# TensorE multiplies an identity by itself 112 times while it waits, in each of five normalizing stages

## The chip, the cores and the metric

The program runs on one core of a Trainium2 chip. The metric is the device time of one execution in microseconds (us), lower is better. The five engines are TensorE (PE), VectorE (DVE), ScalarE (ACT), GpSimd (POOL) and SyncE (SP, which only issues transfers here). TensorE reads its operands from SBUF and writes to PSUM, which has eight banks of 128 x 512 fp32. TensorE's clock has two levels in the profile: a granted clock of 1.00 (2.4 GHz) and of 0.50 (1.2 GHz).

## The reference

A sequence of 512 rows of 1024 numbers (`x`) passes two layers of one kind and then one of another. Everything is fp32.

```python
# each of two layers
h = rms_norm(x, norm1[l])          # x * rsqrt(mean(x*x, over a row) + 1e-6) * gain
proj = h @ w_in[l]                 # four kinds of attention read slices of proj
...
x = x + mixed @ w_out[l]
x = x + square(relu(rms_norm(x, norm2[l]) @ w_up[l])) @ w_down[l]
# then, once
shift, scale, gate = split(silu(c) @ ada_w + ada_b, 3)
h = rms_norm_2(x, norm_w) * (1.0 + scale) + shift
proj = h @ w_in_2                  # gated delta rule and dilated attention follow
```

So rows of x are normalized and multiplied by a weight matrix at five places: twice in each of the two layers, once in the last part. (A final norm of each part isn't followed by a product and uses another function.)

## The kernel before

The kernel is written in stages, one after another. A stage is a block of hand-written programs, one for each engine, with semaphores of its own. It ends in a barrier of all engines (`clear`, L196), and no engine begins the next stage before it. The two layers are a loop on the chip, so their code stands once in the program and runs twice.

Large products take fp32 operands as pairs (a rounded high part and the rest), and each product is three matmuls with 512 moving columns (`product`, L174 to L176). The weights come in items of 512 KB through a ring of four buffers (`WeightRing`). ScalarE makes the high part of an item (L144), VectorE the low part (L153), and TensorE takes both.

`norm_and_turn` is the stage that stands before those products at all five places. Its tile names differ: the rows that it scales are called `proj` (the projecting stage of each layer), `rows_mlp` (the stage ahead of the hidden layer) and `v_t` (the last part), and the pair that it makes is `turned_x`, `turned_x_mlp` and again `turned_x`. Its steps:

1. ScalarE squares the four tiles of x, 128 rows each, and sums them (L274). VectorE makes the mean (L289), ScalarE the root (L276), VectorE its reciprocal (L291).
2. VectorE scales the four tiles and raises `scaled` (L293).
3. TensorE waits for all four (`pe.wait_ge(scaled, T)`), then turns 32 blocks of 128 x 128 through the fp32 identity (L324), four into each of the eight PSUM banks, and raises `turned` once per bank.
4. ScalarE makes the high part of each bank (L280) and VectorE the rest (L298). In the last part there is a bias: VectorE first scales and shifts the bank (L312), ScalarE copies (L283), VectorE subtracts (L302).

`ident_half` is a bf16 copy of the identity, made once at the start. The attention stages use it to add masks (L396). I number the five stages 1 to 5 in the order of time: 1 and 3 are the projecting stages of the two layers, 2 and 4 the stages ahead of the hidden layer, 5 is that of the last part.

Of the kernel before, what the change touches and what calls it, by code (L numbers as in the profile page):

```python
# [32 lines left out]
P = 128  # L33
S = 512
D = 1024
T = S // P
KD = D // P
# [224 lines left out]

def norm_and_turn(nc, psum, x, xn, gains, pair, ident, small, bias=None, work=None):


    ss, ms, root, rstd = (small[:, 4 * i:4 * i + 4] for i in range(4))
    with stage(nc, "squared mean_ready root_ready dve_own scaled turned shifted high low") as (
            squared, mean_ready, root_ready, dve_own, scaled, turned, shifted, high, low), nc.Block() as block:  # L270
        @block.scalar
        def _(act):
            for t in range(T):
                act.activation(xn[:, t, :], x[:, t, :], ACT.Square, accum_out=ss[:, t:t + 1]).then_inc(squared, 1)  # L274
            act.wait_ge(mean_ready, 1)
            act.activation(root, ms, ACT.Sqrt).then_inc(root_ready, 1)  # L276
            for k in range(KD):
                if bias is None:
                    act.wait_ge(turned, k + 1)
                    act.activation(pair[:, k, 0, :], psum[:, k, :], ACT.Copy, scale=gains[:, k:k + 1]).then_inc(high, 1)  # L280
                else:
                    act.wait_ge(shifted, k + 1)
                    act.activation(pair[:, k, 0, :], work[:, k % 2, :], ACT.Copy).then_inc(high, 1)  # L283

        @block.vector
        def _(dve):
            own = Chain(dve, dve_own)
            dve.wait_ge(squared, T)
            dve.tensor_scalar(ms, ss, 1.0 / D, EPS, ALU.mult, ALU.add).then_inc(mean_ready, 1)  # L289
            dve.wait_ge(root_ready, 1)  # L290
            own(dve.reciprocal(rstd, root))  # L291
            for t in range(T):
                dve.tensor_scalar(xn[:, t, :], x[:, t, :], rstd[:, t:t + 1], None, ALU.mult).then_inc(scaled, 1)  # L293

            def rest(k):
                dve.wait_ge(high, k + 1)
                if bias is None:
                    dve.scalar_tensor_tensor(out=pair[:, k, 1, :], in0=psum[:, k, :], scalar=gains[:, k:k + 1],  # L298
                                             in1=pair[:, k, 0, :].bitcast(F32), op0=ALU.mult,
                                             op1=ALU.subtract).then_inc(low, 1)  # L300
                else:
                    dve.tensor_tensor(pair[:, k, 1, :], work[:, k % 2, :], pair[:, k, 0, :].bitcast(F32),  # L302
                                      ALU.subtract).then_inc(low, 1)

            for k in range(KD):
                if bias is None:
                    rest(k)
                    continue
                dve.wait_ge(turned, k + 1)
                if k >= 2:  # L310
                    dve.wait_ge(low, k - 1)
                dve.tensor_scalar(work[:, k % 2, :], psum[:, k, :], gains[:, k:k + 1], bias[:, k:k + 1],  # L312
                                  ALU.mult, ALU.add).then_inc(shifted, 1)
                if k >= 1:
                    rest(k - 1)
            if bias is not None:
                rest(KD - 1)

        @block.tensor
        def _(pe):  # L320
            pe.wait_ge(scaled, T)
            for k in range(KD):
                for t in range(T):
                    mm = pe.transpose(psum[:, k, t * P:(t + 1) * P], xn[:, t, k * P:(k + 1) * P], ident[:])  # L324
                mm.then_inc(turned, 1)
# [337 lines left out]
def layers(nc, psum, x, weights, consts, norm1, w_in, mla_q_norm, mla_kv_norm, mla_w_uq, mla_w_ukv,  # L663
# [8 lines left out]
    with nc.Fori(0, DEPTH) as l, ExitStack() as lay:  # L672
        def sb(name, shape, ctx=lay, dtype=F32):
            return ctx.enter_context(nc.sbuf_tensor(name, shape, dtype))
# [22 lines left out]
        gains = sb("gains", [P, 32])  # L697
# [3 lines left out]
        small = sb("small", [P, 32])  # L701
# [32 lines left out]
        with ExitStack() as mix:  # L734
            values = sb("values", [P, T, VALUES_W], mix)
            gates = sb("gates", [P, 2, S], mix)
            turned = sb("turned_qk", [P, N_TURNED, S], mix)
            with ExitStack() as ctx:
                proj = sb("proj", [P, T, PROJ_W], ctx)
                with ExitStack() as c2:  # L740
                    turned_x = sb("turned_x", [P, KD, 2, S], c2, F32R)

                    rows_x = proj[:].rearrange("p t c -> p (t c)")[:, 0:T * D].rearrange("p (t c) -> p t c", t=T)
                    norm_and_turn(nc, psum, x, rows_x, gains[:, 0:8], turned_x, ident, small)
                    in_projection(nc, psum, weights, turned_x, dict(proj=proj, values=values), turned, chunks, ends,
                                  rope, sb("sines", [P, 896], c2))
                qa = sb("qa", [P, T, 4 * MLA_DIM], ctx)
                ka = sb("ka", [P, T, 4 * MLA_DIM], ctx)
                with ExitStack() as c2:
                    latents(nc, psum, weights, proj, qa, ka, values, gates, gains, forget_bias, gate_forms, small, ident,  # L750
                            rope, sb("latent", [P, T, 384], c2), sb("latent_t", [P, 3, 2, S], c2, F32R),
                            sb("gate_work", [P, 3, S], c2))
                turn_heads(nc, psum, proj, qa, ka, turned, ident)

            chosen = sb("chosen", [P, T, S], mix)
            with ExitStack() as ctx:
                score_keys(nc, psum, values, turned, chosen, causal, sb("relu", [P, 3, S], ctx))
            mixed = sb("mixed", [P, KD, 2, S], mix, F32R)
            with ExitStack() as ctx:
                kept = sb("kept_keys", [P, T - 1, S], ctx, BF16)  # L760
                jobs = layer_jobs(turned, values, gates, kept, causal_half, window, sinks)
                stores = [(mixed[:, c, 0, :], lambda bank: bank, mixed[:, c, 1, :])
                          for g in JOB_ORDER for c in (2 * "abcd".index(g), 2 * "abcd".index(g) + 1)]
                with stage(nc, ATTENTION_SEMS) as sems:
                    attention(nc, psum, jobs, stores, ident, ident_half, sb("probs", [P, 6, S], ctx),
                              sb("probs_t", [P, 2, S], ctx), sb("o_rows", [P, 2, S], ctx),
                              sb("stats", [P, 5, len(jobs)], ctx), sems,
                              besides=(*select_keys(chosen, kept, sb("best", [P, 8], ctx)), 3 * len(jobs) // 8))
            output_products(nc, psum, x, weights, mixed, KD, len(out_items) // 2)


        with ExitStack() as ctx:
            turned_x = sb("turned_x_mlp", [P, KD, 2, S], ctx, F32R)
            with ExitStack() as c2:
                norm_and_turn(nc, psum, x, sb("rows_mlp", [P, T, D], c2), gains[:, 8:16], turned_x, ident, small)
            hidden = sb("hidden", [P, KH, 2, S], ctx, F32R)
            relu = sb("relu_mlp", [P, 3, S], ctx)
            square = sb("square_mlp", [P, 3, S], ctx)
            for half in range(2):
                half_mlp(nc, psum, x, weights, turned_x, hidden, KH, relu, square, len(down_items) // 2)  # L780
# [1397 lines left out]
def second_part(nc, psum, x, weights, consts, a):  # L2178
# [3 lines left out]
    with ExitStack() as all2:  # L2182
        def sb(name, shape, ctx=all2, dtype=F32):
            return ctx.enter_context(nc.sbuf_tensor(name, shape, dtype))
# [19 lines left out]
        small = sb("small_2", [P, 32])  # L2204
        cols = sb("cols_2", [P, 64])
        conv_cols = sb("conv_cols", [P, CONV * 3 * H])
        modulated = sb("modulated", [P, 16])
# [6 lines left out]
        with ExitStack() as ctx:  # L2214
            norm_rows(nc, x, a["final_norm"].rearrange("(o d) -> o d", o=1), sb("norm_work", [P, 3, D], ctx), small)
            work = (sb("vec_rows_2", [64, P], ctx), sb("conv_rows", [96, P], ctx), sb("silu_c", [P, KD], ctx),
                    sb("silu_pair", [P, KD, 2, P], ctx, F32R), sb("gate_bias", [P, D], ctx),
                    sb("mod_rows", [P, 2 * D], ctx))
# [3 lines left out]
        turned_x = sb("turned_x2", [P, KD, 2, S], dtype=F32R)  # L2222
# [6 lines left out]
        with ExitStack() as conv:  # L2229
# [8 lines left out]
            with ExitStack() as ctx:  # L2238
                v_t = sb("v_t", [P, H, S], ctx)
                norm_and_turn(nc, psum, x, v_t[:].rearrange("p k s -> p (k s)").rearrange("p (t c) -> p t c", t=T),  # L2240
                              modulated[:, 0:8], turned_x, ident, small, bias=modulated[:, 8:16], work=scratch)
                with ExitStack() as c2:
                    conv_projection(nc, psum, weights, turned_x, (q_t, k_t, v_t), heads_rows, conv_cols, pick, head_vecs,
                                    (sb("before", [P, 3, S + 3], c2), scratch, sb("soft", [H, 2, S], c2)), n_conv,
# [294 lines left out]
```

## Time and profile before

| | |
|---|---|
| time, median of 3 runs (lowest to highest) | 2691.14 us (2690.57 to 2691.74) |
| profiled execution: its own time | 2687.88 us |
| profiled execution: span | 2686.2 us |
| mean granted TensorE clock over the span | 0.893 |
| TensorE matmuls busy | 2238.1 us (83% of the span) |
| VectorE / ScalarE busy | 1238.2 us (46%) / 862.8 us (32%) |

The span runs from the first to the last instruction of the core, and the execution's own time has 1.7 us around it. A busy share is a mean over stages. What a change in one stage is worth must be read from that stage: which engine the barrier at its end waits for.

### The profile page before, as it was taken

Reading aid. Unit: us, or ns where it says so; the run is one execution under the profiler, and the core shown is the slowest. Engines: PE = TensorE matmul, PEld = TensorE weight load, DVE = VectorE, ACT = ScalarE, POOL = GpSimd, SP = SyncE. Lnnn points to the kernel's source line nnn. Section 1 sums busy time; section 2 is a strip of 40 time slices with the busy share of each in tenths; the row PEclk is TensorE's granted clock in tenths of the full one; section 3 lists DMA queues with packets and bytes.
Section 4 is the critical chain, followed back from the end, with each engine's and each line's share of the span. In section 5 each row is a group of like instructions: output and inputs, shape, how many; then the busy total and the mean of one; then the engine's idle time right before and its main releaser. Section 6 shows DMA issues by size and latency. Waiting matters only on the chain. (4 is left out here: it accounts for less than half of the span.)

```text
span 2686.2 us, 28827 instructions
## 1 busy us (share of the span) xinstructions
PE 2238.1 (83%) x10584; PEld 1780.0 (66%) x10588; DVE 1238.2 (46%) x2313; ACT 862.8 (32%) x1676; POOL 69.1 (3%) x75
## 2 busy tenths in 40 slices
PE   4978988999969968979999965996868785999676
PEld 3866776878857846768878854773756674776454
DVE  2458734323313568434324244665566633224343
ACT  2236423313212255423223133332223224225221
POOL 0000000000000000000000000000012210000000
PEclk9988798999989977789999987996789997998878
DMA  3310021322312300023323244221122223231121
GB/s 104 99 57 1 1 63 57 107 88 87 102 50 84 94 17 1 9 63 94 95 79 94 86 142 143 79 79 32 50 81 75 75 79 134 82 94 33 43 67 47
DMA packets 156565, 192.55 MB, mean 72 GB/s; under 512 B 20555, under 2 KB 118778, under 8 KB 156162
## 3 DMA queue, kind: packets, MB, share of 16 engines
q1 hardware_dynamic: 156418, 190.63, 23.1%
q8 instruction: 87, 1.43, 0.2%
q14 instruction: 60, 0.49, 0.1%
HBM read 178.01 MB, written 12.60 MB: 71 GB/s over the span
## 5 line engine op out<-in xcount | busy, mean ns | idle before, releaser
L153 DVE TENSOR_TENSOR weight_pairs<-weight_ring,weight_pairs 128x1024 fp32r<-128x1024 f32 (+2 forms) x313 | 377.7, 1208 | 642.3 <-ACT weight_pairs L144 641.0
L144 ACT ACTIVATE weight_pairs<-weight_ring 128x1024 fp32r<-128x1024 f32 (+2 forms) x313 | 326.5, 1045 | 803.3 <-PE psum L176 761.5
L174 PE MATMUL psum<-turned_x,weight_pairs 128*128 128x512 f32 (+1 forms) x704 | 292.1, 415 | 38.2 <-PEq L196 24.5
L176 PE MATMUL psum<-turned_x,weight_pairs 128*128 128x512 f32 (+1 forms) x704 | 285.0, 405 | 0.0
L175 PE MATMUL psum<-turned_x,weight_pairs 128*128 128x512 f32 (+1 forms) x704 | 284.1, 404 | 0.0
L174 PE MATMUL psum<-turned_x_mlp,weight_pairs 128*128 128x512 f32 x512 | 204.3, 399 | 13.0 <-PEq L196 13.0
L174 PE MATMUL psum<-weight_pairs,hidden 128*128 128x512 f32 x512 | 203.2, 397 | 0.0
L175 PE MATMUL psum<-turned_x_mlp,weight_pairs 128*128 128x512 f32 x512 | 202.4, 395 | 0.0
L176 PE MATMUL psum<-turned_x_mlp,weight_pairs 128*128 128x512 f32 x512 | 202.3, 395 | 0.0
L176 PE MATMUL psum<-weight_pairs,hidden 128*128 128x512 f32 x512 | 202.0, 395 | 0.0
L175 PE MATMUL psum<-weight_pairs,hidden 128*128 128x512 f32 x512 | 201.8, 394 | 0.0
L174 PEld LDWEIGHTS psum<-turned_x,weight_pairs 128*128 128x128 f32 (+1 forms) x704 | 136.0, 193 | 78.2 <-issue 34.3
L174 PE MATMUL psum<-weight_pairs,turned_x 128*128 128x512 f32 (+2 forms) x384 | 145.9, 380 | 21.7 <-PEq L196 11.3
L176 PEld LDWEIGHTS psum<-turned_x,weight_pairs 128*128 128x128 f32 (+1 forms) x704 | 135.0, 192 | 34.0 <-issue 0.9
L175 PEld LDWEIGHTS psum<-turned_x,weight_pairs 128*128 128x128 f32 (+1 forms) x704 | 135.9, 193 | 31.4 <-issue 0.6
L839 DVE TENSOR_TENSOR square_mlp<-relu_mlp 128x512 f32<-128x512 f32 x64 | 44.1, 689 | 222.4 <-ACT relu_mlp L820 222.4
L176 PE MATMUL psum<-weight_pairs,turned_x 128*128 128x512 f32 (+2 forms) x384 | 144.9, 377 | 0.0
L175 PE MATMUL psum<-weight_pairs,turned_x 128*128 128x512 f32 (+2 forms) x384 | 144.6, 377 | 0.0
L174 PEld LDWEIGHTS psum<-turned_x_mlp,weight_pairs 128*128 128x128 f32 x512 | 96.7, 189 | 36.6 <-issue 14.2
L176 PEld LDWEIGHTS psum<-turned_x_mlp,weight_pairs 128*128 128x128 f32 x512 | 96.8, 189 | 23.7
L176 PEld LDWEIGHTS psum<-weight_pairs,hidden 128*128 128x128 f32 x512 | 96.1, 188 | 24.1
L175 PEld LDWEIGHTS psum<-turned_x_mlp,weight_pairs 128*128 128x128 f32 x512 | 97.1, 190 | 22.2
(404 smaller groups left out, 3620.9 us busy)
## 6 DMA issues: line engine op xcount, KB each, us to landing
weight_ring<-in_w_in_dram SPq DMA_DIRECT2D x104, 512.0 KB, 3.7
weight_ring<-in_w_up_dram SPq DMA_DIRECT2D x64, 512.0 KB, 3.7
weight_ring<-in_w_down_dram SPq DMA_DIRECT2D x64, 512.0 KB, 3.7
weight_ring<-in_w_out_dram SPq DMA_DIRECT2D x24, 512.0 KB, 3.7
weight_ring<-in_ada_w_dram SPq DMA_DIRECT2D x24, 512.0 KB, 4.8
spilled<-v_t SPq DMA_DIRECT2D x22, 256.0 KB, 2.7
weight_ring<-in_w_proj_a_dram SPq DMA_DIRECT2D x8, 512.0 KB, 3.5
qk<-spilled SPq DMA_DIRECT2D x2, 2048.0 KB, 11.6
```

What stands on the lines that cost most here:

```text
L144: act.activation(self.pairs[:, i % SPLIT_RING, 0, 0:n], self.buf[:, i % RING, 0:n], ACT.Copy).then_inc(self.rounded, 1)
L153: dve.tensor_tensor(self.pairs[:, i % SPLIT_RING, 1, 0:n], self.buf[:, i % RING, 0:n], self.pairs[:, i % SPLIT_RING, 0, 0:n].bitcast(F32), ...
L174: pe.matmul(out, lhs[0], rhs[0], start=start, stop=False)
L175: pe.matmul(out, lhs[0], rhs[1], start=False, stop=False)
L176: return pe.matmul(out, lhs[1], rhs[0], start=False, stop=stop)
L839: dve.tensor_tensor(square[:, f % B, :], relu[:, f % B, :], relu[:, f % B, :], ALU.mult).then_inc(squared, 1)
```

## The change

```diff
+IDLE_PRODUCTS = 112
+
+
-def norm_and_turn(nc, psum, x, xn, gains, pair, ident, small, bias=None, work=None):
+def norm_and_turn(nc, psum, x, xn, gains, pair, ident, ident_half, small, bias=None, work=None):
...
         @block.tensor
         def _(pe):
+            for _ in range(IDLE_PRODUCTS):
+                pe.matmul(psum[:, KD - 1, 0:P], ident_half[:], ident_half[:], start=True, stop=True)
             pe.wait_ge(scaled, T)
             for k in range(KD):
                 for t in range(T):
```

The three calls pass `ident_half` on; nothing else changes. Each added matmul comes with a load of its 128 x 128 bf16 weights. All write the same 128 columns of the last PSUM bank, which the turned rows overwrite later; nothing reads them.

On TensorE, around stage 2 and stage 4 (the rows `rows_mlp`; `mixed` belongs to the stage ahead, `turned_x_mlp` with `weight_pairs` to the stage behind), the program had:

```order
L176 MATMUL psum<-weight_pairs,mixed 128x512
L630 UNCONDITIONAL_BRANCH
L319 UNCONDITIONAL_BRANCH [waits barrier_Pool_Activation_PE_DVE_SP_release]
L324 MATMUL psum<-ident,rows_mlp 128x128 [waits scaled]
L324 MATMUL psum<-ident,rows_mlp 128x128 x31
L270 UNCONDITIONAL_BRANCH
L797 UNCONDITIONAL_BRANCH [waits barrier_Pool_Activation_PE_DVE_SP_release]
L174 MATMUL psum<-turned_x_mlp,weight_pairs 128x512 [waits weights_split]
```

and now has (line numbers of the changed file, which are higher by 3 to 5):

```order
L176 MATMUL psum<-weight_pairs,mixed 128x512
L635 UNCONDITIONAL_BRANCH
L322 UNCONDITIONAL_BRANCH [waits barrier_Pool_Activation_PE_DVE_SP_release]
L325 MATMUL psum<-ident_half 128x128 x112
L329 MATMUL psum<-ident,rows_mlp 128x128 [waits scaled]
L329 MATMUL psum<-ident,rows_mlp 128x128 x31
L273 UNCONDITIONAL_BRANCH
L802 UNCONDITIONAL_BRANCH [waits barrier_Pool_Activation_PE_DVE_SP_release]
L174 MATMUL psum<-turned_x_mlp,weight_pairs 128x512 [waits weights_split]
```

The 112 products stand between the barrier's release and the wait for `scaled`, and have no wait of their own. The same row is put in at the same place of the other three stages, and the order of no other engine changes. The chip executes 560 more products in all.

## Rows read from the trace of the kernel before

**Rows 1.** The page: TensorE's busy time, and granted clock in 40 slices.

```profile
PE 2238.1 (83%) x10584; PEld 1780.0 (66%) x10588; DVE 1238.2 (46%) x2313; ACT 862.8 (32%) x1676; POOL 69.1 (3%) x75
...
PEclk9988798999989977789999987996789997998878
```

**Rows 2.** Timeline, stage 2: start, us, engine, line, operation, tiles [idle before it].

```profile
401.42 1.06 ACT L274 ACTIVATE rows_mlp<-x_stream 128x1024 f32<-128x1024 f32 x1 [7.65 <-PEq L196]
...
407.44 2.74 DVE L293 TENSOR_SCALAR rows_mlp<-x_stream,small 128x1024 f32<-128x1024 f32 x4
410.24 5.06 PE L324 MATMUL psum<-ident,rows_mlp 128*128 128x128 f32 x32 [12.06 <-DVE rows_mlp L293]
411.40 0.69 ACT L280 ACTIVATE turned_x_mlp<-psum,gains 128x512 fp32r<-128x512 f32 x1 [4.20 <-PE psum L324]
412.12 5.76 DVE L298 SCALAR_TENSOR_TENSOR turned_x_mlp<-psum,gains,turned_x_mlp 128x512 fp32r<-128x512 f32 x8 [1.93 <-ACT turned_x_mlp L280]
...
418.65 0.47 PE L174 MATMUL psum<-turned_x_mlp,weight_pairs 128*128 128x512 f32 x1 [3.35 <-PEq L196]
```

**Rows 3.** Windows of stage 2: length, busy time of each engine, then clock.

```profile
398.20:402.80 4.60, 0.00 (x0) 0.00 (x0) 2.49 (x4) 1.38 (x3) 0.00 (x0) 1.00 0.02 8
402.80:410.24 7.44, 0.00 (x0) 0.00 (x0) 3.09 (x6) 4.37 (x8) 0.00 (x0) 0.50 0.00 0
410.24:413.04 2.80, 2.80 (x13) 2.80 (x14) 0.82 (x2) 1.37 (x2) 0.00 (x0) 0.50 0.02 6
413.04:418.65 5.61, 2.26 (x22) 2.05 (x20) 4.72 (x7) 3.58 (x6) 0.00 (x0) 1.00 0.00 0
...
419.87:423.28 3.41, 3.41 (x9) 2.67 (x8) 1.14 (x1) 0.00 (x0) 0.00 (x0) 0.50 0.24 61
423.28:430.00 6.72, 6.72 (x30) 5.44 (x29) 0.00 (x0) 1.06 (x1) 0.00 (x0) 1.00 0.13 47
```

**Rows 4.** Timeline, the other four stages.

```profile
23.42 1.28 ACT L274 ACT_TABLE_LOAD   x1 [23.42 <-PEq L196]
33.54 5.66 PE L324 MATMUL psum<-ident,proj 128*128 128x128 f32 x32 [11.35 <-DVE proj L293]
35.42 5.96 DVE L298 SCALAR_TENSOR_TENSOR turned_x<-psum,gains,turned_x 128x512 fp32r<-128x512 f32 x8 [1.93 <-ACT turned_x L280]
...
809.29 6.20 DVE L298 SCALAR_TENSOR_TENSOR turned_x<-psum,gains,turned_x 128x512 fp32r<-128x512 f32 x8 [1.93 <-ACT turned_x L280]
...
1192.83 5.95 DVE L298 SCALAR_TENSOR_TENSOR turned_x_mlp<-psum,gains,turned_x_mlp 128x512 fp32r<-128x512 f32 x8 [1.93 <-ACT turned_x_mlp L280]
...
1646.60 1.06 ACT L274 ACTIVATE v_t<-x_stream 128x1024 f32<-128x1024 f32 x1 [14.83 <-PEq L196]
1655.42 5.39 PE L324 MATMUL psum<-ident,v_t 128*128 128x128 f32 x32 [19.50 <-DVE v_t L293]
```

**Rows 5.** Windows behind the turning in stages 1, 3, 4 and 5.

```profile
44.40:47.80 3.40, 3.30 (x8) 2.63 (x9) 2.31 (x3) 0.68 (x1) 0.00 (x0) 0.50 0.61 169
815.80:822.60 6.80, 3.99 (x9) 3.14 (x10) 3.50 (x3) 2.95 (x3) 0.00 (x0) 0.50 0.40 125
1194.69:1199.54 4.85, 1.78 (x16) 1.57 (x15) 3.98 (x6) 2.98 (x5) 0.00 (x0) 1.00 0.00 0
1199.54:1206.00 6.46, 6.46 (x28) 5.25 (x29) 1.23 (x1) 1.60 (x2) 0.00 (x0) 1.00 0.28 81
1665.70:1672.50 6.80, 2.98 (x8) 0.96 (x9) 4.13 (x7) 2.32 (x3) 0.00 (x0) 0.50 0.37 154
```

**Rows 6.** Matmuls of one line: duration min/median/max in ns.

```profile
L324 PE MATMUL psum<-ident,proj x64: 272/417/477, 33.5 to 813.3; 128*128 128x128 f32 x64
L396 PE MATMUL psum<-causal_half,ident_half x88: 217/229/314, 227.1 to 2451.1; 128*128 128x128 bf16 x88
```

**Rows 7.** Timeline: two pairs of bf16 mask products, at either clock.

```profile
227.08 0.42 PE L396 MATMUL psum<-causal_half,ident_half 128*128 128x128 bf16 x2
235.82 0.28 PE L396 MATMUL psum<-causal_half,ident_half 128*128 128x128 bf16 x2
```

More of the change, by code:

```diff
@@ L743, in layers @@
                     rows_x = proj[:].rearrange("p t c -> p (t c)")[:, 0:T * D].rearrange("p (t c) -> p t c", t=T)
-                    norm_and_turn(nc, psum, x, rows_x, gains[:, 0:8], turned_x, ident, small)
+                    norm_and_turn(nc, psum, x, rows_x, gains[:, 0:8], turned_x, ident, ident_half, small)
                     in_projection(nc, psum, weights, turned_x, dict(proj=proj, values=values), turned, chunks, ends,
@@ L774, in layers @@
             with ExitStack() as c2:
-                norm_and_turn(nc, psum, x, sb("rows_mlp", [P, T, D], c2), gains[:, 8:16], turned_x, ident, small)
+                norm_and_turn(nc, psum, x, sb("rows_mlp", [P, T, D], c2), gains[:, 8:16], turned_x, ident, ident_half, small)
             hidden = sb("hidden", [P, KH, 2, S], ctx, F32R)
@@ L2240, in second_part @@
                 norm_and_turn(nc, psum, x, v_t[:].rearrange("p k s -> p (k s)").rearrange("p (t c) -> p t c", t=T),
-                              modulated[:, 0:8], turned_x, ident, small, bias=modulated[:, 8:16], work=scratch)
+                              modulated[:, 0:8], turned_x, ident, ident_half, small, bias=modulated[:, 8:16], work=scratch)
                 with ExitStack() as c2:
```

## The prediction

> **What bounds the kernel now.** I read the page first: TensorE is busy 83% of the span, and the 40 slices show it at 0.7 to 0.9 of full clock almost everywhere, at 0.9 on the mean [rows 1]. So TensorE's work sets most of the time, and where its clock is low the end moves. Then I read the timeline of one turning stage, stage 2. The chain in it is: ScalarE squares from 401.42, VectorE scales from 407.44 for 2.74 us, TensorE turns from 410.24, ScalarE starts on the first bank at 411.40, VectorE starts at 412.12 and works 5.76 us without a gap to 417.88, and after the barrier the first real product starts at 418.65 [rows 2]. TensorE is idle from the barrier to 410.24, and the new products go into this idle time. They can't shorten the chain up to the scaled rows, on which TensorE has no part.
>
> What they can change is the clock, so I read windows that are cut where the granted clock changes [rows 3]. In stage 2 TensorE has been idle for 4.6 us when its clock falls to 0.50 at 402.80. It comes back to 1.00 at 413.04, 2.8 us after the turning began. It falls again at 419.87, after a gap of 3.35 us and 1.2 us of matmuls, and is back 3.41 us later. So there are two low-clock costs: in the turning, and in the first real products behind it. The change acts directly on the first only.
>
> **Cost of the 560 products.** The room for them is the time from the barrier's release (ScalarE's first instruction shows it) to the first turn. It is 33.54 - 23.42 = 10.1 us in stage 1, the same in stage 3; 410.24 - 401.42 = 8.8 us in stage 2, the same in stage 4; and 1655.42 - 1646.60 = 8.8 us in stage 5 [rows 2, 4].
>
> The trace has no long stream of 128-column bf16 products. The nearest rows are pairs of mask products, which also load 128 bf16 columns each. Two took 0.42 us where one takes 314 ns, so they start 0.11 us apart at the low clock; two took 0.28 us where one takes about 220 ns, so 0.06 us apart at the high one [rows 6, 7]. The bound from above is the fp32 turn, also a load and a 128-column matmul: 2.80 us for 13 is 0.215 us each at the low clock, and 2.26 us for the last 19 is 0.11 us each at the high one (the last one's 272 ns taken off) [rows 3, 6]. I take the pairs, since format and shape are the same. If the clock comes back some 3.8 us after the stream starts (2.8 to 4.0 us was seen here), 35 products pass at 0.11 and 77 at 0.06 to 0.065 us: 3.8 + 4.8 = 8.6 us. That fits into 8.8 and 10.1 us, with little to spare in stages 2, 4 and 5. In stages 2 and 4 the clock may still be high when the stream starts, which leaves more. I cost the products themselves at nothing; the cover is this wait. Without it they would cost 5 x 8.6 = 43 us. The point at which they begin to delay the turning is 8.8 / 112 = 79 ns each on the mean.
>
> The rows have 60 ns at the high clock, but for two products in a row only. The Trainium skill, "TensorE: Matmul & The Clock Gate" (Back-to-back issue gap), has about 81 ns for each load and 128-column matmul in a sustained stream; by it, as an estimate, the 112 would take 9.1 us and the turning would start 0.3 us late in stages 2, 4 and 5. No row here shows such a stream.
>
> **Gain in the turning.** ScalarE begins 1.16 us after the first turn (410.24 to 411.40) [rows 2]. At the high clock three starts of 0.11 instead of 0.215 us, and a fourth turn of 272 instead of up to 477 ns [rows 3, 6], make the first bank ready 0.31 + 0.20 = 0.5 us sooner. Behind that VectorE is the pace: its best run is 5.76 us, 0.72 us a bank [rows 2]. TensorE needs 0.44 us a bank at the high clock and ScalarE 0.69, so VectorE never waits again. Its runs in stages 1, 3 and 4, where TensorE's 0.86 us a bank held them up, took 5.96, 6.20 and 5.95 us [rows 4]. They lose the excess over 5.76: 0.20 + 0.44 + 0.19 = 0.8 us. Stage 5 has two VectorE steps a bank and gains only the start. Sum: 5 x 0.5 + 0.8 = 3.3 us. The turning itself gets over 2 us shorter in each stage, but most of that is no gain: VectorE is late behind it, and TensorE only waits longer at the barrier.
>
> **What the longer gap costs.** The turning ends about 1.5 us sooner in stage 2 and 2 us in stage 4, the real products start 0.5 to 0.7 us sooner, so TensorE's gap between them grows by 1.0 to 1.3 us. A matmul of 512 columns takes 3.41 / 8 = 0.427 us at the low clock and 6.72 / 29 = 0.232 us at the high one [rows 3], so a microsecond at the low clock loses 0.46 us. Behind the turning the kernel paid for 3.3 us in stage 1, 4.0 in stage 3, 3.0 in stage 5 [rows 5], 3.4 in stage 2 [rows 3], and nothing in stage 4, where the matmuls from 1199.54 ran at the high clock [rows 5]. In stages 1, 3 and 5 the clock had fallen before the products began, and a longer gap changes nothing. In stage 2 it falls a little earlier at the same price. Stage 4 came through with 3.1 us of gap where stage 2 with 3.35 did not; with 4.4 us I expect it to fall too, which costs 3.4 x 0.46 = 1.6 us. The ends are 0 and 1.6. Since the gap of stage 4 is so near that of stage 2, other executions of the kernel may have paid it already, and I take half, 0.8 us.
>
> Net: 3.3 - 0.8 = 2.5 us saved. The sum is made against the profiled execution, 2687.88 us, which lies 3.3 us below the median of the runs shown. Taken off the median, it is 2691.14 - 2.5 = **2688.6 us**, or 0.1%. A measurement of this kernel can tell some 0.2% (5.4 us) from no change, so this is "no change that can be told".
>
> **The rivals.**
> - *The clock stays high through the barrier as well.* Then the first real products also run fast, in all stages. The price is the low-clock time behind the turning: (3.3 + 4.0 + 3.0 + 3.4) x 0.46 = 6.3 us more, 2691.1 - 3.3 - 6.3 = 2681.5 us. Against it: after the turning TensorE is idle for 3 to 5 us as before, and the clock fell in four of five stages although it had been high through the second half of the turning. For it: stage 4. Chance 12%.
> - *The products outlast the wait (slower).* Place: the turning starts when the 112 are done and not when the rows are scaled. If the identity doesn't bring the clock back, 0.107 us each makes 12.0 us, late by 1.9 us twice and 3.2 us three times: 13.4 us. The turning then stays slow as well, so nothing is gained: 2704.5 us. At the turns' own 0.11 us it is the same sum less the gain of 3.3 us, 2701 us. It decides above 79 ns a product, and the whole gets slower by over 5.4 us from about 99 ns: then 5 x 112 x 0.099 = 55.4 us exceed the 46.6 us of room by 8.8 us, 3.3 us of which the gain pays back. Chance 8%.
> - *Gain and longer gap cancel, or the turning gains nothing.* This is 2691 us, within 0.5 us. For it: the turning speeds up by itself within 2.8 us, and 0.5 us a stage is all that ScalarE and VectorE can use. Chance 18%. It has a form in the skill. First the row: in stage 2 TensorE did nothing but turn from 410.24, and the clock was at 1.00 from 413.04 [rows 3], so here turning counts as work for the clock. "TensorE: Matmul & The Clock Gate" (Part 4: PE-mode transpose) says that transposes don't engage the high clock. By that rule the turning would drop back between the products and its end, and the 3.3 us would be lost; the row speaks against it.
>
> **How the numbers follow.** The forecast has 62%. With the cancelling case 80% lie within 0.2%, less the edges: I give same 0.77. Faster by over 0.2% takes the clock staying high in most stages: 12% and an edge of 3% of the forecast, 0.15. Slower: 0.08. The forecast's own range is 2686 to 2692 us (from 3.3 us saved and a lucky stage 2, to nothing saved and the turning late by 0.5 us in stages 2, 4 and 5, as it would be if the clock came back only 5 us after the products start). For 8 in 10 it reaches a little to both sides: 2685.0 to 2693.5 us.
>
> **What the changed profile would show.** If I am right: 112 products end before VectorE's fourth scaled tile in each stage; the 32 turns take 3.6 to 3.8 us instead of 5.1 to 6.1; ScalarE's first bank comes 0.65 us after the first turn instead of 1.16; VectorE's run is 5.76 us in all of stages 1 to 4; the real products behind still start at a low clock in four or five stages. The prediction is wrong if TensorE comes late to `scaled`, if the first real products run at 0.23 us in most stages, or if stretches far from these stages change their clock.

## The result and the profile after

The changed kernel took 2672.10 us (median of 8 executions, 2669.5 to 2673.8), the kernel before in the same comparison 2688.03 us (8 executions, 2675.73 to 2691.92). The ratio is 0.9944, with a 95% interval of 0.9929 to 0.9959. I had forecast 2688.6 us with a range of 2685.0 to 2693.5 us, so the prediction was wrong: the kernel got faster by more than the range allows.

Already the 8 executions of before say something that the first three (2690.57 to 2691.74) did not. They range over 16 us. Two later comparisons of the same changed kernel, on two chips, gave ratios of 0.9980 (0.9960 to 1.0000) and 0.9978 (0.9961 to 0.9995). What has to be explained is a gain between 0.2% and 0.56% and a kernel whose own time scatters more than that.

The page of the changed kernel, TensorE's busy time and the clock in 40 slices, to hold against [rows 1]:

```profile
PE 2264.3 (85%) x11148; PEld 1810.3 (68%) x11148; DVE 1236.6 (46%) x2313; ACT 861.9 (32%) x1676; POOL 69.2 (3%) x75
...
PEclk9987799999989977899999987996788997998778
```

The 560 products are there. Next the timeline of stage 2, the stage of [rows 2] (L325 are the new products, L329 the turning, L283 and L301 the two halves of the storing):

```profile
398.54 1.06 ACT L277 ACTIVATE rows_mlp<-x_stream 128x1024 f32<-128x1024 f32 x1 [7.65 <-PEq L196]
398.56 9.03 PE L325 MATMUL psum<-ident_half 128*128 128x128 bf16 x112 [3.25 <-PEq L196]
...
404.57 2.74 DVE L296 TENSOR_SCALAR rows_mlp<-x_stream,small 128x1024 f32<-128x1024 f32 x4
...
407.43 3.66 PE L329 MATMUL psum<-ident,rows_mlp 128*128 128x128 f32 x32
408.07 4.74 ACT L283 ACTIVATE turned_x_mlp<-psum,gains 128x512 fp32r<-128x512 f32 x8 [3.75 <-PE psum L329]
408.79 5.36 DVE L301 SCALAR_TENSOR_TENSOR turned_x_mlp<-psum,gains,turned_x_mlp 128x512 fp32r<-128x512 f32 x8 [1.48 <-ACT turned_x_mlp L283]
...
414.92 0.76 PE L174 MATMUL psum<-turned_x_mlp,weight_pairs 128*128 128x512 f32 x1 [3.83 <-PEq L196]
```

The windows of the same stage, cut where the clock changes, against [rows 3]:

```profile
398.54:404.08 5.54, 5.52 (x53) 5.54 (x54) 0.17 (x1) 5.52 (x9) 0.00 (x0) 0.50 0.02 4
404.08:407.43 3.35, 3.35 (x63) 3.35 (x61) 2.92 (x5) 0.23 (x2) 0.00 (x0) 1.00 0.00 0
407.43:411.09 3.66, 3.66 (x35) 3.42 (x32) 2.30 (x4) 3.02 (x6) 0.00 (x0) 1.00 0.00 0
411.09:414.32 3.23, 0.00 (x0) 0.00 (x0) 3.06 (x5) 1.72 (x3) 0.00 (x0) 1.00 0.00 0
414.32:417.74 3.42, 2.82 (x7) 2.27 (x8) 1.23 (x1) 1.06 (x1) 0.00 (x0) 0.50 0.02 5
417.74:424.00 6.26, 6.26 (x29) 5.06 (x28) 0.00 (x0) 1.06 (x1) 0.00 (x0) 1.00 0.27 84
```

Read from the top: the products run at 0.50 for 5.5 us (about 107 ns each), then at 1.00 (56 ns each), and end so close to the scaled rows that the turning has no idle time ahead of it. The whole turning is at 1.00 and takes 3.66 us instead of 5.06. But the clock falls at 414.32, just ahead of the first real product, and stays low for 3.42 us, as it did before at 419.87. Stage 4, whose first real products ran at the high clock before [rows 5], now has a low stretch of 6.83 us, which begins ahead of the first real product at 1187.12:

```profile
1185.73:1192.56 6.83, 5.44 (x13) 4.31 (x14) 1.84 (x2) 1.06 (x1) 0.00 (x0) 0.50 0.25 75
```

In all five stages, from ScalarE's first square to the first real product: 18.75, 16.38, 18.73, 16.38 and 22.40 us, where before took 19.78, 17.23, 20.01, 17.41 and 22.92. That is 4.7 us sooner in sum. To the start of the 40th real matmul the sum is only 1.7 us better (147.6 against 149.3 us): these forty took 3.0 us longer, in stages 1 and 4 above all, and 20.4 instead of 13.8 us of them lay at the low clock. The spans, however, differ by 2686.2 - 2670.8 = 15.4 us. Cut at the first squares of the five stages, the two stretches that hold the layers' attention stages gave 2.6 and 8.2 us, the one behind stage 5 gave 3.3 us (what the five stages gave themselves is in these figures). So most of the difference arose where the program had not been changed.

### The profile page after: what moved, and what is told of

Its sections match the earlier page's. It is cut to its first block and busy times, and to the rows that moved or that the text cites. A ratio compares the mean times of both kernels' runs of the same rounds, so it can differ in the third digit from the quotient of the medians.

```text
span 2670.8 us, 29951 instructions
## 1 busy us (share of the span) xinstructions
PE 2264.3 (85%) x11148; PEld 1810.3 (68%) x11148; DVE 1236.6 (46%) x2313; ACT 861.9 (32%) x1676; POOL 69.2 (3%) x75
## 5 line engine op out<-in xcount | busy, mean ns | idle before, releaser
L175 PE MATMUL psum<-turned_x_mlp,weight_pairs 128*128 128x512 f32 x512 | 203.1, 397 | 0.0
L174 PEld LDWEIGHTS psum<-turned_x_mlp,weight_pairs 128*128 128x128 f32 x512 | 97.4, 190 | 38.0 <-issue 15.4
```

The costliest lines, as they stand in the source:

```text
L174: pe.matmul(out, lhs[0], rhs[0], start=start, stop=False)
L175: pe.matmul(out, lhs[0], rhs[1], start=False, stop=False)
```

## The experiments

Each kernel is an edit of one of the two, had 12 executions and was compared with 23 to 35 of before on its chip. Where I count executions "above 2682 us", the limit is moved by the delay that a kernel adds (twice per program). A few executions lie near the limit; what changes with another limit is said below the table.

**e1, the kernel before again** (no edit).

> The kernel before, unchanged, to see what its time and its low-clock stretches do by themselves. In the two profiles at hand the five turning stages account for only 4.7 us less up to the first real product and 3.0 us more behind it; most of the 15.4 us between the spans arises in the attention stages, where TensorE's clock was low at other moments. Theory A (attention's clock is scatter that has nothing to do with the products): the time scatters between 2676 and 2692 us, and this second profile has its low stretches in attention at other places than the first. Theory B (the products fix attention's clock by moving the work): the time stays at 2685 to 2692 us and the profile has the same low stretch of about 41 us near 1055 us as the first.

Measured: 2672.76 to 2695.3 us, median 2685.29, ratio 0.9999 (0.9978 to 1.0020). Over all comparisons the kernel before was executed 171 times: 67 times above 2682 us (mean 2688 us), 104 times below (median 2676.2 us). So its time has a lower group around 2676 us and an upper one that spreads from 2682 to 2698 us. The profile of e1 shows both kinds of attention in one execution, in the windows here. The first two rows are the attention stages of layers 1 and 2 as a whole; then come the low stretches of layer 1 (two), those of layer 2 (two), and the high stretch behind these:

```profile
227.00:349.30 122.30, 109.16 (x696) 80.79 (x696) 95.19 (x301) 65.24 (x217) 0.00 (x0) 0.83 0.00 1
1000.58:1130.59 130.01, 117.95 (x696) 85.77 (x696) 95.39 (x301) 65.08 (x217) 0.00 (x0) 0.78 0.00 1
265.20:278.80 13.60, 12.93 (x56) 9.26 (x56) 12.03 (x40) 7.45 (x28) 0.00 (x0) 0.50 0.00 1
292.50:309.50 17.00, 14.76 (x64) 10.90 (x66) 13.64 (x37) 6.42 (x21) 0.00 (x0) 0.50 0.00 1
1036.60:1046.80 10.20, 9.08 (x41) 6.59 (x40) 8.82 (x29) 6.10 (x23) 0.00 (x0) 0.50 0.00 1
1053.60:1094.50 40.90, 39.47 (x154) 25.57 (x154) 30.23 (x82) 13.08 (x44) 0.00 (x0) 0.50 0.00 1
1094.50:1128.70 34.20, 32.09 (x248) 25.23 (x248) 15.09 (x47) 20.12 (x62) 0.00 (x0) 1.00 0.01 1
```

The same 696 matmuls took 122.3 us in one layer and 130.0 us in the other. VectorE and ScalarE did the same work (95 and 65 us). In the slow one TensorE was busy for 39.5 of 40.9 us at the low clock, so almost nothing covered its slowness (in the fast layer it was busy for 12.9 of 13.6 and 14.8 of 17.0 us). The times are those that theory A expected. The low stretch near 1055 us is again there in layer 2, while layer 1 has others than in the first profile, so the profile alone doesn't decide.

Over the 20 profiles (40 attention stages) of this study the stage, from its first mask product to the first product of the next stage, took only a few lengths. They go with the moments at which the clock changes. Every one of these stages begins in a low stretch; the third column says when that one ends, the last has the next ones:

| length of attention, us | how often | first rise, us from the start | next low stretches, us from the start |
|---|---|---|---|
| 122.0 to 122.4 | 24 | 7.0-7.6 | 37.7-38.3 to 51.3-51.9, 65.0-65.6 to 82.0-82.6 |
| 123.2 | 1 | 7.0 | 37.7 to 51.3, 54.8 to 78.6 |
| 124.6 to 124.7 | 9 | 8.4-8.5 | 35.7-35.8 to 80.1-80.2, without a break |
| 130.0 | 4 | 5.2-5.3 | 36.0 to 46.2, 53.0 to 94.0 |
| 134.7 | 2 | 5.1-5.2 | 35.9 to 46.1, 52.9 to 104.1 |

The moment of the next fall makes up to 12 us: at 37.7 us or later the stage took 122 or 123 us, at 36.0 us or earlier 124.6 to 134.7. The moment of the first rise tells the long ones ahead of time: all six stages of 130 us and more, and no other, have it at 5.1 to 5.3 us. All five profiled executions of more than 2686 us have a layer with 130 us or more, and of the other fifteen only e17 (below) has one.

**e2, products in stages 1 and 3 only; e3, in 2 and 4 only; e4, in 5 only.** The edits, with the count as an argument of each call:

```diff
-            for _ in range(IDLE_PRODUCTS):
+            for _ in range(idle):     # e2: 112, 0, 0   e3: 0, 112, 0   e4: 0, 0, 112
```

> The 112 products in stages 1 and 3 only. Theory A (each stage gives its own clock gain, attention is scatter): 1.0 to 1.3 us sooner to the first real product in each, so 0 to 3 us less than before. Theory B (attention is decided by what stands ahead of it in the layer, which is stages 1 and 3): 10 to 13 us less than before, most of it in the attention stages of the two layers.

> The 112 products in stages 2 and 4 only. Theory A: 0 to 2 us less than before. Theory B: little in layer 1's attention, which stands ahead of stage 2; up to 8 us in layer 2's attention and in the last part behind stage 4.

> The 112 products in stage 5 only, where the real products came 0.5 us sooner in the changed kernel. Theory A: within 1 us of before. Theory B: up to 3 us less, all behind 1655 us, since the span behind stage 5 was 3.3 us shorter in the changed profile.

Measured: e2 2675.87 us median (2672.34 to 2678.97), ratio 0.9976 (0.9961 to 0.9991), none of 12 above 2682 us. e3 2686.05 us, 1.0010 (0.9987 to 1.0032), 8 of 12 above. e4 2686.79 us, 1.0016 (0.9994 to 1.0038), 9 of 12 above. The share of the upper group is gone with products in stages 1 and 3 alone, and stays without them. The 10 to 13 us that theory B expected of e2 are not there on the median, since on this chip most executions of before are in the lower group: what vanishes is the group, not a fixed time. So the stages ahead of attention in the same layer are the ones that matter. A count of twelve alone is weak evidence: e1 is the kernel before and had 7 of 12, while before had 12 of 35 on the same chip. The argument rests on the counts of all kernels together, below the table.

**e5 and e18, the changed kernel again.**

> The changed kernel once more. The kernel before, repeated, took 2672 to 2695 us in two groups (near 2676 and near 2687), and the changed one 2669.5 to 2673.8 in eight runs. Theory A (attention's clock is chance, the same for both): its times now reach 2685 us and more too, and the medians differ by 1 to 4 us. Theory C (products in stages 1 and 3 keep the slow attention from occurring): all runs stay below 2680 us, as with products in stages 1 and 3 only (2672.3 to 2679.0).

> The changed kernel once more, beside e17. If products that last until the turning keep the slow attention away: all 12 executions below 2682 us, median 2672 to 2677, and the median of the kernel before on this chip 1 to 5 us above it.

Measured: e5 2676.37 us (2670.69 to 2679.91), none above 2682 us; e18 2673.73 us (2671.38 to 2683.8), one above. With the first comparison 1 of 32 executions is in the upper group, against 67 of 171.

The profile of e18 also shows where 112 products end too early, in stage 2:

```profile
397.37 6.41 PE L325 MATMUL psum<-ident_half 128*128 128x128 bf16 x112 [3.25 <-PEq L196]
```

Here the clock was still high at the barrier. The products passed in 6.41 us, the clock fell 2.5 us after them, just as the turning began at 406.18, and the turning took 5.38 us.

**e6, products behind the turning too; e17, and ahead of the first weights.** The edit to the changed kernel:

```diff
                 mm.then_inc(turned, 1)
+            pe.wait_ge(low if bias is None else shifted, 1)
+            for _ in range(48 if bias is None else 144):
+                pe.matmul(psum[:, 0, 0:P], ident_half[:], ident_half[:], start=True, stop=True)
...
+            for _ in range(36):     # e17 only, first thing in in_projection
+                pe.matmul(psum[:, KD - 1, 0:P], ident_half[:], ident_half[:], start=True, stop=True)
```

> The changed kernel with more products behind the turning: 48 in stages 1 to 4 and 144 in stage 5, so that TensorE works while ScalarE and VectorE store the last banks. The theory of my prediction (the low clock of the first real products comes from the gap behind the turning, and costs 0.46 us per us) says: the first real products start at the high clock in stages 2, 4 and 5, up to 1.5 us less in each, 3 to 5 us less in sum. The rival (the gap to the barrier and weights is still too long, or attention decides all) says no change against the changed kernel.

> As e6 (112 products ahead of the turning, 48 or 144 behind it), and 36 more at the start of the projecting stages, where TensorE waits 2.4 us for the first weights. If the low clock behind the turning is what takes the gain back: the first real products of all stages run at the high clock, 3 to 6 us less than the changed kernel, no execution above 2682 us. If attention's moment alone decides: the median is that of the changed kernel or the slow group is back.

Measured: e6 2672.76 us (2667.45 to 2683.72), ratio to before 0.9962 (0.9938 to 0.9987), against 2676.37 us of e5 on the same chip. e17 2672.30 us (2662.75 to 2680.15), 0.9970 (0.9951 to 0.9989), against 2673.73 us of e18. Their medians are 3.6 and 1.4 us below the changed kernel's on the same chip, the lowest of this study beside the first comparison's, though the intervals against before overlap with those of the changed kernel. The timeline of e6 in stage 2 (L333 are the new products behind the turning), and then its windows from the first product on:

```profile
411.41 2.84 PE L333 MATMUL psum<-ident_half 128*128 128x128 bf16 x48
...
415.41 0.47 PE L174 MATMUL psum<-turned_x_mlp,weight_pairs 128*128 128x512 f32 x1 [1.16 <-PEq L196]
```

```profile
399.03:414.20 15.17, 12.75 (x192) 12.47 (x192) 8.01 (x14) 10.49 (x18) 0.00 (x0) 1.00 0.01 2
414.20:415.41 1.21, 0.06 (x1) 0.03 (x1) 0.44 (x1) 0.00 (x0) 0.00 (x0) 1.00 0.00 0
415.41:424.55 9.14, 9.14 (x40) 7.39 (x40) 1.22 (x1) 2.12 (x2) 0.00 (x0) 1.00 0.19 59
```

The gap that was 3.83 us is 1.16 us, the clock stays at 1.00, and the 40th real matmul starts 9.14 us after the first. In e6 the clock still fell in stage 3, at 813.46, ahead of the first real product there. In e17 the first 40 ran at the high clock in all five stages, in 9.0 to 9.2 us each. So that part of the theory is shown. The profiled execution of e17 nevertheless has an attention stage of 130.0 us in layer 2 and took 2673.6 us:

```profile
990.38:1120.38 130.00, 117.96 (x696) 85.77 (x696) 95.37 (x301) 65.18 (x217) 0.00 (x0) 0.78 0.00 1
```

Bridging saves time where it is done, and it doesn't keep the long attention away. Not all that is saved there arrives at the end: from the first squares to the 40th real matmuls the five stages sum to 141.1 us in e6 and 138.3 in e17, against 148.6 in e5 and 147.8 in e18, which is 7.5 and 9.5 us less, while the medians are 3.6 and 1.4 us lower. Part of it is the other attention stages of these profiles (2.5 and 5.5 us longer in sum), the rest is open.

**e7, e13, e11, e15, a delay without products; e12, a delay ahead of the layers.** The kernel before, with work on ScalarE ahead of the squares of stages 1 and 3. The buffer is overwritten later:

```diff
+            for d in range(delay):      # e7: 1   e11: 2   e15: 3   e13: the first line once
+                act.activation(pair[:, d, 0, :], x[:, 0, 0:S], ACT.Square)
+                act.activation(pair[:, d, 1, :], x[:, 0, 0:S], ACT.Square)
```

> The kernel before with two more squares of 128x512 on ScalarE ahead of stages 1 and 3, about 1.2 us of pure delay in each and no product. Theory A: about 2.4 us more than before, two groups as before. Theory D (where attention falls against the clock's changes is what matters, and any shift in stages 1 and 3 changes it): the share of executions above 2682 us changes markedly, up or down.

> The kernel before with a delay of about 0.53 us (one square of 128x512) in stages 1 and 3. Executions above 2682 us plus twice the delay, so above 2683 us, count as slow. If the share follows the shift, it lies between the 38 of 105 without a delay and the 10 of 12 with 1.05 us. If the 10 of 12 were chance, it is a third.

> The kernel before with twice the delay (2.1 us) in stages 1 and 3. One delay put 11 of 12 executions above 2682 us. Theory D: again another share, either way, beside the 4.2 us of the delay itself. Theory A (chance): two groups as before, shifted by 4.2 us.

> The kernel before with a delay of 3.15 us in stages 1 and 3; above 2688.5 us counts as slow. If the share follows the shift it is again another one; if a delay doesn't matter, a third.

> The kernel before with the two squares of the delay once, in a stage of its own ahead of the two layers (about 1.1 us and one more barrier), so the lengths of stages 1 and 3 are unchanged. If the slow attention depended on the time since the start of the program, its share changes, as with the delay in stages 1 and 3. If it depends on the time from one layer's stages to the next, the share stays at a third to a half and the time rises by 2 to 4 us.

In the profile of e7 the delay is 25.82 - 24.77 = 1.05 us. In that of e12, whose two squares stand in a stage of their own ahead of both layers, the first square of stage 1 starts at 27.85 instead of 24.72, so 3.1 us later; its count in the table is the same with the limit moved by 3.1 us.

```profile
24.77 0.63 ACT L274 ACTIVATE turned_x<-x_stream 128x512 fp32r<-128x512 f32 x1
25.30 0.61 ACT L275 ACTIVATE turned_x<-x_stream 128x512 fp32r<-128x512 f32 x1
25.82 1.04 ACT L277 ACTIVATE proj<-x_stream 128x1024 f32<-128x1024 f32 x1
```

**e9, three squares of half width, no products; e10, e14, e16, products in stages 1 and 3 and a delay.** e9 makes stages 1 and 3 shorter by leaving out three halves of the row sums (so its results are not those of the reference). e10, e14 and e16 are e2 with the lines of e7, e13 and e11.

```diff
-                act.activation(xn[:, t, :], x[:, t, :], ACT.Square, ...)
+                w = S if t < narrow else D      # e9: narrow = 3 in stages 1 and 3
+                act.activation(xn[:, t, 0:w], x[:, t, 0:w], ACT.Square, ...)
```

> The kernel before, without products, but three of the four squares in stages 1 and 3 take only the first 512 columns, so three halves of the row sums are left out and the rows are scaled some 1.3 us sooner. Theory D (the slow attention depends on how long stages 1 and 3 take, not on what TensorE does in them): the slow group above 2682 us vanishes, as it does with the products. Theory C (it takes products and a high clock in the turning): a third to a half of the executions stay above 2682 us, and the rest is 2.6 us less.

> Products in stages 1 and 3 only, and ahead of the squares in these stages the delay of 1.05 us on ScalarE, so that the first real product comes about when it does in the kernel before. Theory D: the slow group comes back, a third to a half of the executions above 2682 us. Theory C: no execution above 2682 us, all about 2 us above those with products in stages 1 and 3 only (2672 to 2679).

> Products in stages 1 and 3 only, with the delay of 0.53 us in them. If the products protect by themselves: at most 1 of 12 above 2683 us. If the shift alone decides: some delay between 0 and 3 us must bring the slow group back also with products, and this is one try.

> Products in stages 1 and 3 only, with the delay of 2.1 us in them; above 2686 us counts as slow. If the products protect by themselves: at most 1 of 12. If the shift alone decides: the slow group may come back, since with this delay the first real product comes over 1 us later than in the kernel before.

**e8, 48 products instead of 112.**

> The changed kernel with 48 instead of 112 products in all five stages; they end 4 to 5 us after the barrier, so TensorE is idle for 4 to 6 us before the turning. Theory of the clock in the turning: in most stages the clock has fallen again when the turning starts, so the first real product comes hardly sooner than before, and the gain is under 2 us. Theory C by number: whatever products in stages 1 and 3 do for attention needs a high clock in the turning, so the slow group comes back.

The results of these, in one table. "Upper" is the number of 12 executions above the moved limit; the ratio is to before.

| what stages 1 and 3 have | kernel | median, us | ratio (95% interval) | upper |
|---|---|---|---|---|
| 1.3 us shorter | e9 | 2675.74 | 0.9989 (0.9961 to 1.0017) | 4 (above 2679.4) |
| nothing | e1 | 2685.29 | 0.9999 (0.9978 to 1.0020) | 7 (before: 67 of 171) |
| 0.53 us delay | e13 | 2688.38 | 1.0034 (1.0012 to 1.0057) | 10 |
| 1.05 us delay | e7 | 2690.20 | 1.0029 (1.0004 to 1.0053) | 10 |
| 2.1 us delay | e11 | 2685.71 | 1.0029 (1.0011 to 1.0047) | 5 |
| 3.15 us delay | e15 | 2690.72 | 1.0046 (1.0027 to 1.0066) | 7 |
| nothing, a delay ahead of both layers | e12 | 2684.07 | 1.0027 (1.0003 to 1.0052) | 6 |
| 112 products | e2 | 2675.87 | 0.9976 (0.9961 to 0.9991) | 0 |
| 112 products, 0.53 us delay | e14 | 2676.15 | 0.9996 (0.9978 to 1.0015) | 1 |
| 112 products, 1.05 us delay | e10 | 2678.59 | 0.9996 (0.9976 to 1.0015) | 1 |
| 112 products, 2.1 us delay | e16 | 2691.14 | 1.0034 (1.0011 to 1.0058) | 7 |
| 48 products | e8 | 2677.16 | 0.9987 (0.9966 to 1.0009) | 3 |

Without products every length of the stages has an upper group, of a third to five sixths. Whether a shift alone changes the share isn't shown: e7 and e13 have 20 of 24, but e1, e3 and e4, which have no shift in stages 1 and 3, have 24 of 36. No shift tried removes the group; e9, which starts the real products sooner as the change does, still has 4. With products and up to 1.05 us of delay 2 of 36 executions are in it. With 2.1 us of delay it is back.

All kernels together say it more firmly. The nine comparisons of a kernel with no products in stages 1 and 3 (e1, e3, e4, e7, e9, e11, e12, e13, e15) each have 4 to 10 of 12 in the upper group, 66 of 108. The eight with 112 products there and at most 1.05 us of delay (the changed kernel three times, e2, e6, e10, e14, e17) each have none or one, 4 of 92. With the limit 2 us lower it is 70 against 7, with 2 us more 60 against 2, so the limit doesn't decide it.

The profile of e16 shows what is different there, in stage 1 (L329 the products, L333 the turning), and then the window from the products' end and that from the first turn on:

```profile
23.65 7.68 PE L329 MATMUL psum<-ident_half 128*128 128x128 bf16 x112 [1.25 <-PEq L196]
35.82 5.38 PE L333 MATMUL psum<-ident,proj 128*128 128x128 f32 x32 [4.48 <-DVE proj L300]
```

```profile
31.34:35.82 4.48, 0.00 (x1) 0.01 (x1) 3.04 (x6) 1.42 (x2) 0.00 (x0) 1.00 0.00 0
35.82:40.01 4.19, 4.19 (x23) 4.19 (x24) 2.62 (x4) 3.00 (x5) 0.00 (x0) 0.59 0.00 0
```

The delay leaves 4.5 us of idle time between the products and the turning, the clock falls 0.8 us after the turning has begun (so 0.59 on the mean of that window), and the turning takes 5.38 us, nearly what it takes without products. In e8 it is the same from another side: 48 products end at 27.7 us, the turning begins at 33.60 and takes 5.16 us. Its 3 of 12 can't be told from the 39% of before. What e2, e10 and e14 have in common, and e16 and e8 have not, is a short gap: in their profiles the products of stages 1 and 3 end 1.5 to 2.4 us before the turning, in e16 3.1 and 4.5, in e8 4.8 and 5.9 us. In five of the six stages of e2, e10 and e14 the turning was at the high clock throughout. In stage 1 of e2 it was not, although the execution took 2673.7 us:

```profile
23.54 7.84 PE L326 MATMUL psum<-ident_half 128*128 128x128 bf16 x112 [1.10 <-PEq L196]
33.62 5.24 PE L330 MATMUL psum<-ident,proj 128*128 128x128 f32 x32 [2.25 <-DVE proj L297]
```

The profiles are too few to tie the long attention to the turning itself: it followed 1 of 15 turnings at the high clock (stage 3 of e17) and 5 of 25 others.

A second observation fits. From the end of the first square to the first real product, stages 1 and 3 take 17.7 us wherever the turning is at the high clock throughout. Where part of it is at the low clock they take 18.2 to 19.3 us, depending on when the clock changes (e9, whose stage is shortened, left aside).

## Why the prediction was wrong

**The cost of the products: right.** The pairs' rows gave 0.11 and 0.06 us a product; measured were 107 and 56 ns in a stream. They took 8.0 to 9.2 us where 8.6 was forecast. The wait for the clock was read too short: "2.8 to 4.0 us was seen here" leaves out stage 3, where 4.98 us passed from the first turn to the rise (807.42 to 812.40), and in the changed profile it took 5.5, 5.9 and 5.2 us from the first product in stages 2, 3 and 5. The forecast still held, because in stage 4 the clock was high first and the products at the high clock took 56 and not 60 to 65 ns. They delayed the turning only where it was tightest (by about 0.07 us in stage 2, nothing in stage 1). The "products outlast the wait" rival did not occur, and a stream pitch of 81 ns, as the Trainium skill's page "TensorE: Matmul & The Clock Gate" (Back-to-back issue gap) has it, is not what this chip did.

**The gain in the turning: right in kind, too small.** I had 3.3 us, it was 4.7. ScalarE's first bank came 0.64 to 0.70 us after the first turn in stages 1 to 4 (forecast 0.65). The term that was mis-sized is the 5.76 us of VectorE's run, which I took for its floor: in the changed profile it takes 5.36 us in all of stages 1 to 4, 1.6 us less in sum. The row of before merges eight instructions. Their starts in the trace are 0.85 and 0.86 us apart at first, TensorE's pace at the low clock, and 0.66 to 0.67 us after that, so the best run of before still held two waits.

**The longer gap: right in kind, too small.** I took 0.8 us, of ends at 0 and 1.6. In the two profiles it was 3.0 us: 2.5 in stage 4, which ran high before and now has a low stretch of 6.8 us from 1185.73, 1.2 in stage 1, and 0.6 less in the others together. The 1.2 us of stage 1 can't be put down to the change, since e1, the kernel before again, has a low stretch of 6.83 us there too and is as slow (11.8 us from the first to the 40th). Net of both, the two profiles have 1.7 us to the 40th matmul. The other profiles bear it out: 149.3 and 150.2 us in those of before and e1, 147.6, 148.6 and 147.8 us in those of the changed kernel, e5 and e18, so again 1.7 us between the means. The executions agree: in the lower group the mean goes from 2675.8 to 2674.1 us, where 2.5 us was forecast.

**The step that failed is the scope of the sum.** "What they can change is the clock, so I read windows": I read them around the five stages only, and took the rest of the program as fixed, and the three executions of 2690.57 to 2691.74 us as its time. Neither holds. Attention takes 122 to 135 us by the moment of the clock's changes, and all three were in the upper group, so the forecast was taken off a base some 10 us too high and left out the term that moved most. The mean of all executions goes from 2680.6 (171) to 2674.4 us (32), 6.2 us or 0.23%. Of it 1.7 us is the lower group's, and the rest is the upper group: (0.39 - 0.03) x 12.2 us = 4.4 us. The 0.56% of the first comparison is larger because 7 of its 8 executions of before happened to be in the upper group. My sentence that 0.2% can be told from no change was wrong for the same reason: with 8 or 12 executions the group shares alone move a median by several us. The last of my three signs of a wrong prediction, "if stretches far from these stages change their clock", is what occurred.

**The rivals.** "The clock stays high through the barrier as well" gave the measured sign but not the cause: the clock fell behind the turning in all five stages of the profile. e17 shows what it is worth when forced, 9.0 to 9.2 us for the first 40 matmuls of a stage instead of 10.4 to 11.9. "Gain and longer gap cancel" was nearer to what the stages did, 4.7 against 3.0 us in the two profiles, but it is not what decided the time. The Trainium skill's rule in Part 4 of the same page, that transposes don't engage the high clock, is contradicted as it was in the rows of before: in stage 1 of e16 and of e8 TensorE only turned from the fall or the first turn on, and the clock rose during it, at 40.01 and 36.62 us.

**What stays open.** That products which last until 2.4 us or less before the turning lower the share of the upper group is shown by counts (2 of 36 in e2, e10, e14, 1 of 32 in the changed kernel). That the executions of the upper group are those with a long attention stage is what the profiles show, with e17 as the exception. By which steps products 190 us earlier keep attention's start away from the bad moment is open. An argument would be that a turning at the high clock makes the stage's length constant, and so narrows the moments at which attention can begin. The profiles don't bear it out: from the first square to attention's first mask product it is 198.7 to 201.7 us where the turning was at the high clock, and 201.6 to 203.1 us where it was not (e9 left aside). That is earlier, but not narrower. And e9, which is earlier too (200.6 and 200.8 us) without products, has the upper group. e17 shows that the products are no guarantee. I did not separate layer 1 from layer 2, which share their code.

## What to carry to other kernels

If a kernel's engines alternate between one being the bound and another, TensorE's clock is part of the state that a stage hands to the next: compare several profiles of the same kernel, stage by stage, before a difference far from the edit is put down to it, and look at the distribution of the times, not at three that agree. Filler products are worth most when they end right at the wait they fill, and the gap behind the short burst deserves them as much as the gap ahead (e6's median was 3.6 us below the change alone on its chip, with intervals that overlap). A pure delay of the same stage without the edit's work is the cheapest control for "it only moved things".

## What was unexpected of the hardware

- The same 696 matmuls of attention take 122.0 to 122.4, 124.7, 130.0 or 134.7 us, with the clock's next fall at 37.7 us or later in the first, and at 35.7 to 36.0 us in the others. The stages of 134.7 us differ from those of 130.0 in that the second low stretch lasts until 104 and not 94 us.
- The same kernel, run twice side by side, had medians of 2685.3 us (e1, 12 executions) and 2678.2 us (35 executions) on one chip.
- Bf16 loads and products of 128 columns in a stream of 112 start 56 ns apart at the high clock and 107 ns at the low one.
